# Stage borders of a one-core hybrid decoder: pair order, first fetches, causal masks and a late norm strip

## The reference, cut to what matters

```python
for layer A:
    u = rms_norm(x, mix_norm[0]) @ a_w_in           # r, k, v, and the inputs of decay, rate, gate
    w = tanh(wd) @ w_up ; a = sigmoid(a0 + ad @ a_up) ; g = sigmoid(gd) @ g_up
    main = rwkv7(u, w, a) * g
    x = x + concat(main, memory_attention) @ w_out[0]
    x = x + swiglu(rms_norm(x, ffn_norm[0]), w_gate_up[0], w_down[0])
k, v, c = shared_kv(x)                               # w_kv; keys normed per head; c = cumsum of log f
for layer B:
    u = rms_norm(x, mix_norm[1]) @ b_w_in            # 12 query heads, 12 gate heads, 4 memory heads
    s = q k^T * scale + c_q - c_k, -1e30 above the diagonal
    main = softmax(s) v * sigmoid(gate)
    x = x + concat(main, memory_attention) @ w_out[1]
    x = x + swiglu(rms_norm(x, ffn_norm[1]), w_gate_up[1], w_down[1])
```

## Time and profile before

| what | value |
|---|---|
| runs shown | 3070.31, 3073.22, 3076.67 us; median 3073.22 |
| profiled execution | 3074.48 us, its span 3072.7 us |
| mean granted TensorE clock | 0.965 of full |
| PE busy | 2831.5 us, 92% |
| weight loads (PEld) | 2278.5 us, 74% |
| DVE busy | 1561.8 us, 51% |
| POOL busy | 1159.1 us, 38% |
| ACT busy | 1073.1 us, 35% |
| HBM read, written | 186.80 MB, 70.83 MB |

### The profile page before, as it was taken

The page is one execution under the profiler, slowest core; times in us unless marked ns, Lnnn a source line. Parts: engine busy times, 40 slices in busy tenths (PEclk is TensorE's granted clock), DMA queues, the critical chain, the costliest instruction groups (busy, mean ns, idle before and its releaser), DMA issues. The chain is left out here.

```text
span 3072.7 us, 55169 instructions
## 1 busy us (share of the span) xinstructions
PE 2831.5 (92%) x23253; PEld 2278.5 (74%) x23253; DVE 1561.8 (51%) x2127; ACT 1073.1 (35%) x1876; POOL 1159.1 (38%) x1037
## 2 busy tenths in 40 slices
PE   7999688888869899999999999959989999999998
PEld 5888467777648788888887777736657788888887
DVE  6233355666542745555324778747742755544322
ACT  3111233333241533333103766635542533333000
POOL 5354033333223444445433554411102544444432
PEclk9999789999989999999999999979999999999999
DMA  5332200000014132224423232243113132224321
GB/s 198 106 103 83 95 16 24 24 24 31 3 49 144 55 110 83 82 83 128 148 77 100 56 102 91 76 137 116 71 41 112 49 113 86 85 85 160 115 72 66
DMA packets 265422, 261.19 MB, mean 85 GB/s; under 512 B 9366, under 2 KB 221452, under 8 KB 264024
## 3 DMA queue, kind: packets, MB, share of 16 engines
q1 hardware_dynamic: 258664, 236.02, 24.3%
q10 hardware_dynamic: 6032, 21.61, 2.0%
q0 software_dynamic: 480, 0.03, 0.0%
HBM read 186.80 MB, written 70.83 MB: 84 GB/s over the span
## 5 line engine op out<-in xcount | busy, mean ns | idle before, releaser
L303 POOL TENSOR_TENSOR w_lo_b<-w_raw_b,w_hi_b 128x512 fp32r<-128x512 f32 (+1 forms) x500 | 667.2, 1336 | 508.3 <-ACT w_hi_b L335 494.7
L385 PE MATMUL ps<-b_hi,w_hi_b 128*128 128x512 f32 x1540 | 607.6, 395 | 7.7 <-issue 4.1
L385 PE MATMUL ps<-b_hi,w_lo_b 128*128 128x512 f32 x1540 | 600.6, 390 | 0.0
L385 PE MATMUL ps<-b_lo,w_hi_b 128*128 128x512 f32 x1540 | 600.6, 390 | 0.0
L385 PEld LDWEIGHTS ps<-b_hi,w_hi_b 128*128 128x128 f32 x1540 | 289.9, 188 | 73.4 <-issue 8.3
L385 PEld LDWEIGHTS ps<-b_lo,w_hi_b 128*128 128x128 f32 x1540 | 289.9, 188 | 63.0 <-issue 3.6
L385 PEld LDWEIGHTS ps<-b_hi,w_lo_b 128*128 128x128 f32 x1540 | 289.8, 188 | 60.5
L299 POOL CAST w_hi_b<-w_raw_b 128x384 fp32r<-128x384 f32 (+2 forms) x170 | 99.6, 586 | 526.1 <-PE ps L357 307.5
L335 ACT ACTIVATE w_hi_b<-w_raw_b 128x512 fp32r<-128x512 f32 x330 | 205.9, 627 | 246.3 <-DVE w_raw_b L322 123.9
L357 PE MATMUL ps<-b_hi,w_hi_b 128*128 128x512 f32 x784 | 244.0, 393 | 18.3 <-DVE b_lo L2660 15.6
L357 PE MATMUL ps<-b_lo,w_hi_b 128*128 128x512 f32 x784 | 243.3, 392 | 0.0
(11 more groups left out here) (332 smaller groups left out, 5288.4 us busy)
## 6 DMA issues: line engine op xcount, KB each, us to landing
w_raw_b<-in_w_gate_up SPq DMA_DIRECT2D x88, 512.0 KB, 4.2
act_dram<-x_res SPq DMA_DIRECT2D x44, 512.0 KB, 6.0
stage<-act_dram ACTq DMA_DIRECT2D x32, 512.0 KB, 3.5
w_raw_b<-in_w_down SPq DMA_DIRECT2D x32, 384.0 KB, 3.7
w_raw_a<-in_a_w_in SPq DMA_DIRECT2D x23, 512.0 KB, 4.7
u_dram<-evac_a SPq DMA_DIRECT2D x23, 512.0 KB, 3.0
w_raw_b<-in_w_down SPq DMA_DIRECT2D x32, 320.0 KB, 3.1
w_raw_b<-in_w_out SPq DMA_DIRECT2D x16, 512.0 KB, 5.7
```

The lines of the kernel that those rows point to most:

```text
L303: nc.gpsimd.tensor_tensor(self.wlo[:, r, 0:n, :], source, self.whi[:, r, 0:n, :].bitcast(F32), ALU.subtract).then_inc(self.w_lo, 1)
L385: mm = self.nc.tensor.matmul(self.ps[:, bank, :], w[:, r, k, :], h[:, block, k, :], start=(start and k == 0 and a == 0 and h is self.bh), ...
```

## The change

Four places change. (1) `PROJ_PAIRS`: (head 12, head 13) moves from place 12 to place 10; the sigmoid of pair 13's first gate is issued ahead of ACT's copy of the last product; and SP loads two more strips of the output projection ahead of pair 12's stores. (2) The recurrence fetches `lora` and `up_wa` first, then k, v, r of pair 0, then the gate's four tensors, on a semaphore of their own; the two gate sigmoids stand behind the sigmoids of decay and rate. (3) POOL masks tile by tile, 128 columns in each instruction, in the order of use. (4) Strip 7 of the output projection is stored with a semaphore that outlives the stage; its square, its sum into `acc` and its multiplication by the norm weights are made within the gate-up stage, and PE sums `acc` before the sixth strip instead of the third.

```diff
 PROJ_PAIRS = ([(("keys", c), ("vt", PAIRS + c)) for c in range(PAIRS)] + [(("head", 0), ("head", 1))]
-              + [(("head", 2 + i), ("gate", PAIRS + i)) for i in range(4)] + [(("head", 12), ("head", 13)), (("gate", 10), ("gate", 11))])
+              + [(("head", 2 + i), ("gate", PAIRS + i)) for i in range(2)] + [(("head", 12), ("head", 13))]
+              + [(("head", 4 + i), ("gate", PAIRS + 2 + i)) for i in range(2)] + [(("gate", 10), ("gate", 11))])
...
-                    while at < len(loads) and loads[at] <= self.units[u0 + p + 2].strips[-1]:
+                    while at < len(loads) and loads[at] <= self.units[u0 + p + (2 if p < N else 4)].strips[-1]:
...
+                    if p == N:
+                        open_gate(N, 0)
                     act.wait_ge(self.block_done, j + 7)
                     snap(p, 1, 0, b)
                     ahead(6)
-                for i in range(2):
-                    open_gate(N, i)
+                open_gate(N, 1)
...
-                for dst, src in ((lora[:], self.u_dram[18]), (gate0[:], self.u_dram[19]), (gate1[:], self.u_dram[20][0:32, :]),
-                                 (up_wa[0:HD, :], ins["a_w_up"][0]), (up_wa[HD:P, :], ins["a_a_up"][0]),
-                                 (up_g0[:], ins["a_g_up"][0][0:P, :]), (up_g1[:], ins["a_g_up"][0][P:160, :])):
+                for dst, src in ((lora[:], self.u_dram[18]), (up_wa[0:HD, :], ins["a_w_up"][0]), (up_wa[HD:P, :], ins["a_a_up"][0])):
                     sp.dma_start(dst, src).then_inc(lora_in, 16)
...
                     sp.dma_start(r[:, p % 2, :], self.u_dram[p]).then_inc(r_in, 16)
+                    if p == 0:
+                        for dst, src in ((gate0[:], self.u_dram[19]), (gate1[:], self.u_dram[20][0:32, :]),
+                                         (up_g0[:], ins["a_g_up"][0][0:P, :]), (up_g1[:], ins["a_g_up"][0][P:160, :])):
+                            sp.dma_start(dst, src).then_inc(gates_in, 16)
...
-                act.wait_ge(lora_in, 7 * 16)
-                nc.scalar.activation(lora[0:HD, :], lora[0:HD, :], ACT.Tanh)
-                nc.scalar.activation(gate0[:], gate0[:], ACT.Sigmoid)
-                nc.scalar.activation(gate1[:], gate1[:], ACT.Sigmoid).then_inc(lora_ready, 1)
+                act.wait_ge(lora_in, 3 * 16)
+                nc.scalar.activation(lora[0:HD, :], lora[0:HD, :], ACT.Tanh).then_inc(lora_ready, 1)
                 decay_sigmoid(0)
                 rate_sigmoid(0)
+                act.wait_ge(gates_in, 4 * 16)
+                nc.scalar.activation(gate0[:], gate0[:], ACT.Sigmoid)
+                nc.scalar.activation(gate1[:], gate1[:], ACT.Sigmoid).then_inc(gates_ready, 1)
                 kk_square(0)
...
-                    for h in range(2):
-                        nc.gpsimd.tensor_tensor(decay_masked[:, p % 2, h, :].rearrange("p (t c) -> p t c", t=TT),
-                                                decay[:, p % 2, h, :].rearrange("p (t c) -> p t c", t=TT), future, ALU.add).then_inc(masked, 1)
+                    for _, t in units[TT * p:TT * (p + 1)]:
+                        at = slice(t * P, (t + 1) * P)
+                        for h in range(2):
+                            nc.gpsimd.tensor_tensor(decay_masked[:, p % 2, h, at], decay[:, p % 2, h, at], future, ALU.add).then_inc(masked, 1)
...
-                        if n % TT == 0:
-                            dve.wait_ge(masked, 2 * (p + 1))
+                        dve.wait_ge(masked, 2 * (n + 1))
...
-                for k in range(KT):
+                for k in range(KT - 1):
                     act.wait_ge(self.psum_free, k + 1)
...
                 for k in range(KT):
+                    if k == 2:
+                        nc.scalar.activation(staged(1), X[:, KT - 1, :], ACT.Square).then_inc(self.squared, 1)
+                    if k == KT - 1:
+                        act.wait_ge(self.strip_kept, 16 * (l + 1))
+                        act.wait_ge(self.squared, 1)
+                        nc.scalar.activation(X[:, k, :], X[:, k, :], ACT.Copy, scale=self.param(f"ffn_norm{l}", k)).then_inc(self.squared, 1)
+                        act.wait_ge(self.squared, 2)
                     copy(blocks_of(bh, k), two(X[:, k, :])).then_inc(self.h_hi, 1)
...
                 for k in range(KT):
+                    if k == 3:
+                        dve.wait_ge(self.squared, 1)
+                        tt(acc, acc, staged(1), ALU.add).then_inc(self.added, 1)
                     dve.wait_ge(self.h_hi, k + 1)
...
-                    if k == 2:
+                    if k == 5:
+                        pe.wait_ge(self.added, 1)
                         for t in range(TT):
```

More of the change, by code:

```diff
@@ L411, in build @@
             self.w_gain = ctx.enter_context(nc.semaphore("w_gain"))
+            self.strip_kept = ctx.enter_context(nc.semaphore("strip_kept"))
             self.x_last = [ctx.enter_context(nc.semaphore(f"x_last{r}")) for r in range(2)]
@@ L1305, in phase_rwkv @@
             gmat, hmat, rbar = sb("gmat", [P, 4, C]), sb("hmat", [P, 4, C]), sb("rbar", [P, 4 * C])
-            lora_in, mem_in = sem("lora_in"), sem("mem_in")
+            lora_in, mem_in, gates_in, gates_ready = sem("lora_in"), sem("mem_in"), sem("gates_in"), sem("gates_ready")
             kv_in, r_in = sem("kv_in"), sem("r_in")
@@ L1420, in gate_product @@
                     cols = slice(p * P, (p + 1) * P)
+                    pe.wait_ge(gates_ready, 1)
                     pe.wait_ge(kk_used, 2 * min(p + 1, PAIRS - 1) + j + 1)
@@ L2044, in _ @@
             def _(pool):
-                future = self.const("future").rearrange("p (a c) -> p a c", a=1).broadcast_to([P, TT, P])
+                future = self.const("future")
                 for p in range(PAIRS):
@@ L2362, in phase_out_and_ffn @@
             self.phase_begins(f"out{l}")
-            kept = [self.sem(f"kept{k}") for k in range(KT)]
+            kept = [self.sem(f"kept{k}") for k in range(KT - 1)]
             block = ctx.enter_context(nc.Block())
@@ L2374, in _ @@
                         sp.wait_ge(self.psum_free, i)
-                        sp.dma_start(self.x_dram[:, i - 1, :], self.X[:, i - 1, :]).then_inc(kept[i - 1], 16)
+                        sp.dma_start(self.x_dram[:, i - 1, :], self.X[:, i - 1, :]).then_inc(kept[i - 1] if i < KT else self.strip_kept, 16)
                     if i < len(loads):
@@ L2404, in _ @@
                     nc.vector.tensor_tensor(self.X[:, i, :], self.X[:, i, :], self.bank2(i % 3), ALU.add).then_inc(self.psum_free, 1)
-                    if i >= 1:
+                    if 1 <= i < KT - 1:
                         dve.wait_ge(self.squared, i + 1)
@@ L2608, in _ @@
                         if k >= 2:
-                            act.wait_ge(self.added, k - 1)
+                            act.wait_ge(self.added, k)
                         nc.scalar.activation(acc if k == 0 else staged(1), X[:, k, :], ACT.Square).then_inc(self.squared, 1)
@@ L2647, in next_sums @@
                     dve.wait_ge(self.h_lo, KT + k + 1)
-                    dve.wait_ge(self.squared, k + 1)
+                    dve.wait_ge(self.squared, k + 3)
                     if k < HK:
@@ L2719, in _ @@
                             if c:
-                                dve.wait_ge(self.squared, c + 1)
-                                dve.wait_ge(self.added, c - 1)
+                                dve.wait_ge(self.squared, c + 3)
+                                dve.wait_ge(self.added, c)
                                 tt(acc, acc, staged(1), ALU.add).then_inc(self.added, 1)
```

## The result

The changed kernel takes **3051.60 us** (median of 4 runs, 3049.29 to 3055.99) against 3071.76 (3067.50 to 3076.67) measured beside it: ratio 0.9936, 95% interval 0.9923 to 0.9948. The same kernel was measured twice more: 3057.40 (7 runs, ratio 0.9952, 0.9935 to 0.9969) and 3056.64 (5 runs, 0.9963, 0.9949 to 0.9976). Over all 16 runs it is 15.2 us faster than the kernel before beside it (means; standard error 1.3). So about 5 of the surplus of 8.35 are the draw of the first four runs. The other 3.4 is what is left to explain.

A forecast was written before the change was run, and what follows sets the result against it. PE, busy for 92% of the span, was taken as dense inside stages and idle at their borders. Terms -5.0 - 3.6 - 9.6 + 3.35 + 3.0 + 0 = -11.85 gave 3061.5 us, range 3055 to 3068.5.

The forecast's parts named there:

- the costing of the recurrence: Start of the recurrence: earlier fetches save 5.0 us, which carries through the one chain up to the loop.
- Recurrence start: Recurrence's fetches: PE starts at 348.6, `kk_square` at 357.9 instead of 363.14; -5.0 us, ends -5.6 and -3.6.
- First masks: Start of the forgetting attention: DVE needs only two 128-column masks, 0.52 us each, and starts 3.6 us earlier.
- The later masks are therefore hidden: Forgetting attention: POOL's sixteen masks take 8.4 us in a pair of 34.7, so those after the first cost nothing.
- End of the projections: Border from projections to attention: less work and earlier strip loads behind PE's last product; -9.6 us, ends -11.1 and -8.
- Price of the pair of two heads: Projections, place 10: a PE wait of +3.35 us and +3.0 for the half clock.
- Gate-up: Entry to gate-up, both layers: PE starts 3.45 us sooner but waits longer later; 0 each, ends -1.9 and +1.5.
- Gate-up pays in full: Rival: DVE's sums start 3.45 us earlier in both gate-up layers, giving 3054.6 us; chance 0.10.
- Masks make POOL the bound: Rival in the attention: small masks cost 2.91 us each, deciding from 2.17; +71, about 3137 us; chance 0.02.
- The projections give nothing: Rival: delayed attention fetches and longer half clock make the projections' edit worth 0, giving 3064.7 us; chance 0.17.
- Smaller gains at several borders: Rival: several borders gain less at once, or half clock comes somewhere new, giving 3064 to 3070 us; chance 0.09.

The follow-up runs named there:

- c_only: Kernel before with the recurrence's fetch edit alone, PE waiting for the gates ahead of each of 12 gate products: 3058.28 us against 3071.01.
- c_one_wait: Kernel before with the recurrence's fetch edit alone, PE waiting for the gates once instead of 12 times: 3065.82 us against 3071.01.
- pad_only: Kernel before with only 12 PE waits that never hold, one ahead of each gate product, no fetch moved: 3069.64 us against 3071.01.
- a_only: Kernel before with the projections' edit alone: 3065.62 us against 3071.01.
- d_only: Kernel before with the tile-by-tile masks alone: 3072.02 us against 3073.39.
- root_later: Changed kernel with DVE's wait for the root and its reciprocal moved behind sums T1 and T2 in gate-up: 3053.81 us against the kernel before's 3073.39.
- after_one_wait: Changed kernel with PE waiting for the gates once instead of 12 times: 3062.32 us against the kernel before's 3073.39.
- first12: Changed kernel with all 12 gate waits ahead of the first gate product: 3063.09 us against the kernel before's 3073.74.

## Why the prediction was wrong

**The step that failed** is the costing of the recurrence: "Everything behind it up to the loop is one chain, so it carries through", and behind that the 24 steps were taken to move as a block. The 12 waits for the gates, the only edit inside the steps, have no term: they were put at nothing without a reason. They never hold after the first, but the runs give them -7.5 (c_only against c_one_wait), -3.4 with a standard error of 1.6 (the changed kernel against its forms without spread waits) and -1.4 to -3.4 (pad_only). That the waits do it is shown by the first of these pairs and borne out by the others; how they do it is argued. In the profiles it goes with PE's fetch of instructions: where the waits stand spread, the last step mostly has no gap (7 of 9 profiles, 1 of 11 otherwise), and its clock mostly stays at 2.4 GHz for longer. The rest of the distance was the draw of the first four runs: 16 runs give -15.2, which would have been in the range.

**The terms**, from stretches of all profiles that hold or lack the edit:
- *Recurrence start*, -5.0: measured -3.9 in the stretch of the first two profiles, -4.4 over all (65.9 on average in 14 profiles with the edit, 70.3 in six without), -5.2 by c_one_wait's runs. PE's start at 346.74 looks better than the 348.6 forecast, but the stage before ended 3.1 earlier in this profile: it is 14.3 behind that end, and 13.05 was forecast. `kk_square` came at 356.10, 7.0 earlier and 3.9 of it here. The term is right to within a microsecond; what it had too low is the landing. `up_wa` landed 4.9 us after its issue began, near the 5.3 of the earlier trace rows and not the 3.7 that the prediction took. The Trainium skill's 2.0 us and bytes ("DMA: Bandwidth & Descriptors", anatomy of one DMA), by which the prediction's estimate was -5.7, is further off; that section measures transfers which GpSimd issues, and SP issued these.
- *First masks*, -3.6: measured -3.7 at the place (5.21 against 8.88), a mask 0.46 on average where 0.52 was said. But from the last product of the projections to the end of the attention only -0.7 (232.1 on average in 12 profiles, against 232.8 in a_only) to +0.4 (243.2 in d_only, against 242.8) is left, -1.4 in runs. The sentence "The later masks are therefore hidden" was right of POOL and left out DVE, whose wait stands ahead of every tile now: the wait was an addition without a price, too.
- *End of the projections*, -9.6: measured -10.1 (the same stretch: 232.8 in a_only against 242.8 on average in six profiles without the edit, 241.3 to 244.3).
- *Price of the pair of two heads*, +6.35: measured +4.8 (309.1 on average in seven profiles with the old order, 313.9 in ten with the new one; without root_later's 311.1 it is +5.1). The wait is the 3.35 that was forecast; the half clock behind it (3.4 us long in the changed kernel's first profile, 6.8 in the model pair 7) cost some 1.5 instead of 3.0.
- *Gate-up*, 0: measured +0.4 for both layers. The wait of 2.66 is the forecast's "2 to 4 us", and the half clock that the range allowed for came behind it.
- Together -11.85 forecast; after_one_wait, which has all four edits and no spread waits, took -11.1. That sum comes out so near because errors cancel: the masks gave 2 to 4 less than their term, the price of the pair was 1.5 lower and the end of the projections 0.5 better.

**The rivals.** *Gate-up pays in full* gave 3054.6, nearest to the first result by its number, and is wrong by its mechanism. *Masks make POOL the bound* is out (0.46 for a mask, where it needed 2.17). *The projections give nothing* is out (-5.4 by a_only). *Smaller gains at several borders* held of the masks alone.

**What stays open**: why the position of waits decides when a piece of the program is asked for. It is not the position alone: in the last step first12 has PE's program exactly as far on as the changed kernel, and has the gap. And equal kernels differ in it from one execution to the next: in step 1 the changed kernel's first profile has no gap, its other two have one.

## What to carry to other kernels

Count every added wait as an edit, on the engine that bounds the stage most of all: twelve of which eleven or all never hold moved this kernel by -1.4 to -7.5 us on PE, and one for each tile on DVE, as far as the comparison of two profiles shows, gave back most of what the finer masks had won. Where one wait gives the guarantee, test both forms. An edit of less than 5 us can't be judged here from one profile or four runs; compare the stretch that it changes over several profiles, and take the time from a dozen runs.

## What the runs showed of the hardware

- PE can stand for 0.8 to 1.4 us in the middle of a dense stretch with no semaphore late (step 1, ten profiles). In the last step such a gap (0.9 to 1.6 us) ends 2.3 to 2.7 us behind the start of a transfer of the queue for instructions. The code ahead of it was small matmuls, 156 records in the step's first 5 us in after_one_wait.
- In a stretch where PE is already thin (busy for 62% and 67% of the last step in the two profiles shown) the half clock came 15 us sooner with such a gap than without (7.2 and 22.5 us in). Over all profiles the step was 4.3 longer with the gap (33.4 in 12, 29.1 in 8).
- A DVE wait that finds its semaphore long raised seems to cost too: with it, 0.27 instead of 0.17 us went by ahead of the same DVE instruction, and PE's waits for DVE were 0.1 longer.
